# Two-block transformer kernel, one Trainium2 core: 36 of 44 up-projection pairs of the convolution feed-forward as seven half-size block products, with GpSimd making the weight sums, the gated product and its remainder

## The reference, cut to what matters

```python
def conv_ffn(h, w_up, conv_w, conv_b, w_down):
    u = h @ w_up                       # 512 x 1024 by 1024 x 5632
    u = lax.conv_general_dilated(u, conv_w[:, None, :], window_strides=(1,),
        padding=[(CONV_WIDTH - 1, 0)], feature_group_count=c, ...) + conv_b
    a, gate = jnp.split(u, 2, axis=-1)
    return (jax.nn.silu(gate) * a) @ w_down     # 512 x 2816 by 2816 x 1024
...
h = rms_norm_2(x, ffn_norm_g[layer])
x = x + conv_ffn(h, ffn_w_up[layer], ffn_conv_w[layer], ffn_conv_b[layer], ffn_w_down[layer])
```

## Time and profile before

| What | us |
|---|---|
| Time, median of 3 runs (lowest, highest) | 3203.16 (3202.86, 3203.87) |
| Span of the profiled execution, first to last instruction | 3201.8 |
| PE busy | 3186.1 |
| DVE busy | 1969.6 |
| ACT busy | 1271.3 |
| POOL busy | 404.6 |

### The profile page before, as it was taken

The page is one execution under the profiler, slowest core; times in us unless marked ns, Lnnn a source line. Parts: engine busy times, 40 slices in busy tenths (PEclk is TensorE's granted clock), DMA queues, the critical chain, the costliest instruction groups (busy, mean ns, idle before and its releaser), DMA issues.

```text
span 3201.8 us, 44978 instructions
## 1 busy us (share of the span) xinstructions
PE 3186.1 (100%) x16214; PEld 2672.4 (83%) x16214; DVE 1969.6 (62%) x2804; ACT 1271.3 (40%) x1734; POOL 404.6 (13%) x356
## 2 busy tenths in 40 slices
PE   9999999999999999999999999999999999999998
PEld 7788888889998788888889998768888888888887
DVE  8455567585557455557585555666665744585656
ACT  4433333334453433343334453254332523553423
POOL 2100000124221100000124221051000101320001
PEclk9999999999999999999999999999999999999999
DMA  7146324423323156324423322203222322122222
GB/s 267 67 167 206 126 94 167 140 92 106 106 99 106 55 169 208 121 98 166 142 87 106 106 99 83 86 21 112 99 99 93 105 99 92 47 85 100 92 99 79
DMA packets 100037, 359.24 MB, mean 112 GB/s; under 512 B 11056, under 2 KB 13360, under 8 KB 99760
## 3 DMA queue, kind: packets, MB, share of 16 engines
q1 hardware_dynamic: 98960, 354.08, 32.3%
q0 software_dynamic: 928, 3.17, 0.3%
HBM read 355.11 MB, written 2.10 MB: 112 GB/s over the span
## 4 chain that ended last, share of the span: by engine, by line
PE 94%; DVE 2%; POOLq 1%; issue 1%; ACT 1%; DVEq 1%; DMA 0%; ACTq 0%; SPq 0%; POOL 0%
PE pb L687 21%; PE pb L688 21%; PE pb L689 21%; PE pb L1002 6%; PE pb L719 2%; PE pb L720 2%; PE pb L723 2%; PE pb L759 2%; PE pb L757 2%; PE pb L758 2%; PE pb L1110 1%; PE pb L1485 1%; PE pb L1486 1%; PE pb L1487 1%; PE pb L978 1%
## 5 line engine op out<-in xcount | busy, mean ns | idle before, releaser
L1557 ACT ACTIVATE hi<-raw 128x1024 fp32r<-128x1024 f32 x500 | 524.8, 1056 | 850.0 <-PE pb L689 543.5
L2181 DVE TENSOR_TENSOR lo<-raw,hi 128x1024 fp32r<-128x1024 f32 (+1 forms) x500 | 617.6, 1241 | 330.1 <-ACT hi L1557 304.3
L687 PE MATMUL pb<-yH,hi 128*128 128x512 f32 (+1 forms) x1664 | 644.2, 387 | 0.0
L688 PE MATMUL pb<-yL,hi 128*128 128x512 f32 (+1 forms) x1664 | 644.0, 387 | 0.0
L689 PE MATMUL pb<-yH,lo 128*128 128x512 f32 (+1 forms) x1664 | 643.9, 387 | 0.0
L687 PE MATMUL pb<-hH,hi 128*128 128x512 f32 x1128 | 440.5, 391 | 0.0
L688 PE MATMUL pb<-hL,hi 128*128 128x512 f32 x1128 | 439.0, 389 | 0.0
L689 PE MATMUL pb<-hH,lo 128*128 128x512 f32 x1128 | 438.9, 389 | 0.0
L687 PEld LDWEIGHTS pb<-yH,hi 128*128 128x128 f32 x1664 | 312.5, 188 | 63.6
L689 PEld LDWEIGHTS pb<-yH,lo 128*128 128x128 f32 x1664 | 312.4, 188 | 63.5
L688 PEld LDWEIGHTS pb<-yL,hi 128*128 128x128 f32 x1664 | 312.5, 188 | 63.4
(11 more groups left out here) (486 smaller groups left out, 5237.5 us busy)
## 6 DMA issues: line engine op xcount, KB each, us to landing
raw<-stream SPq DMA_DIRECT2D x648, 512.0 KB, 3.3
yF<-first SPq DMA_DIRECT2D x8, 512.0 KB, 12.0
act<-first SPq DMA_DIRECT2D x8, 512.0 KB, 16.5
x<-xT SPq DMA_DIRECT2D x4, 512.0 KB, 7.6
outT<-act SPq DMA_DIRECT2D x7, 256.0 KB, 2.2
act<-crow POOLq DMA_DIRECT2D x2, 512.0 KB, 5.6
tab<-decay SPq DMA_DIRECT2D x1, 1024.0 KB, 7.8
scr<-ws POOLq DMA_DIRECT2D x2, 256.0 KB, 3.1
```

The lines of the kernel that those rows point to most:

```text
L687: pe.matmul(out, whi, ahi, start=first, stop=False)
L688: pe.matmul(out, whi, alo, start=False, stop=False)
L1557: act.activation(hi[:, s], raw[:, s], ACT.Copy).then_inc(hi_ready, 1)
L2181: dve.tensor_tensor(lo[:, s, 0:width], raw[:, s, 0:width], hi[:, s, 0:width].bitcast(F32), ALU.subtract).then_inc(lo_ready, 1)
```

## The change

`CONV_FAST = (4, 8, 6)` pairs at the end of the three slabs go through `conv_group` in place of two plain tiles: 18 pairs a layer, 36 in the kernel. The first 4 pairs of the first slab of a layer stay plain. In detail:

- **PE** runs `seven_products`, the routine of the first block's groups made general. It waits for `lo_ready` of the two tiles, for `e_lo` (the rest of the weight sums) and for `p_kept` (copies out of PSUM by ACT).
- **GpSimd** first makes the token sums (`conv_tokens`: 8 `tensor_scalar` of 512 columns and 16 `tensor_tensor` of 256). Then, for each fast pair, it makes four weight sums (`four_sums`, one of them in place in `raw`), and the product `a` by `gate` and the rest `midL` of the pair two back in its list, which were DVE's.
- **ACT** gets four copies of 256 columns out of PSUM for each fast pair and a rounding of 128x1536 sums, beside what it had.
- **DVE** gets the rest of the sums (128x1536), and two instructions for every plain one on PSUM: an addition that reads PSUM and then a multiplication by `rows`, SBUF by SBUF. It no longer makes the product nor `midL`, but for the last pair of a slab.
- The three `hi` and `lo` that a slab's down tiles start with are made at three places inside the last fast pair (`tick(1)`, `tick(2)`, `tick(3)`).

Buffers `ext` and `extR` are new (6 x 512 floats a partition), and the kernel asks for a `dynamic_dma_scratch_size` of 4096. The core of the diff, without the removed lines of the old `fast_group`:

```diff
+CONV_FAST = (4, 8, 6)
+FAST_1 = 2 * len(FAST_SLABS) * FAST_GROUPS
...
+        c_sum = lambda q: act3[:, 4:7] if q else ext[:, 0:3]
+        c_sumL = lambda q: halved[:, 4:7] if q else extR[:, 0:3]
+        c_sumH = lambda q: tabR[:, 1:4] if q else extR[:, 3:6]
+        c_kept = lambda q, i: scr[:, q * S + i * 256:q * S + (i + 1) * 256]
+        c_at = lambda layer, j, m: FAST_1 + layer * sum(CONV_FAST) + sum(CONV_FAST[:j]) + m - (SLABS[j] - CONV_FAST[j])
+        c_kept_at = lambda at: 3 * FAST_1 + 4 * (at - FAST_1)
...
+            def four_sums(at, n, sums):
+                if at >= 2:
+                    pool.wait_ge(p_full, 5 * (at - 1))
                 pool.tensor_tensor(e3, a11, a21, ALU.subtract)
                 pool.drain()
                 pool.tensor_tensor(a21, a21, a22, ALU.add)
...
+            def conv_pairs(layer):
+                conv_tokens(layer)
+                for j, n in enumerate(SLABS):
+                    first = n - CONV_FAST[j]
+                    def sums_of(m):
+                        e = c_sum(m % 2)
+                        four_sums(c_at(layer, j, m), c_tile(layer, j, m), [e[:, i] for i in range(3)])
+                    def product_of(m):
+                        pool.wait_ge(gated, layer * sum(SLABS) + sum(SLABS[:j]) + m + 1)
+                        p = A[:, 2 * m % RING]
+                        pool.tensor_tensor(p, p, A[:, 2 * m % RING + 1], ALU.mult)
+                        pool.drain().then_inc(product, 1)
+                        pool.wait_ge(product_hi, layer * (sum(SLABS) - 3) + sum(SLABS[:j]) - j + m + 1)
+                        pool.tensor_tensor(midL[:, m], p, midH[:, m].bitcast(F32), ALU.subtract)
+                        pool.drain().then_inc(y_ready, 1)
+                    sums_of(first)
+                    for m in range(first, n):
+                        if m + 1 < n:
+                            sums_of(m + 1)
+                        if m:
+                            product_of(m - 1)
...
+            def seven_products(at, q, banks_of, own, token, extra, kept_at, before_token=None, before_upper=None):
+                s0, s1 = 2 * q, 2 * q + 1
+                one_sum, other_sum, upper, lower_sum = (pb[:, b, 0:256] for b in banks_of)
                 pe.wait_ge(lo_ready, tiles.next())
                 pe.wait_ge(bank_free, banks.next(2))
+                product_of(one_sum, ring_part(s0, 0), own(0, 0)).then_inc(p_full, 1)
                 pe.wait_ge(lo_ready, tiles.next())
+                if before_token is not None:
+                    pe.wait_ge(t_lo, before_token)
+                product_of(other_sum, ring_part(s1, 0), token(1)).then_inc(p_full, 1)
+                if before_upper is not None:
+                    pe.wait_ge(y_ready, before_upper)
+                product_of(upper, ring_part(s0, 1), own(1, 0)).then_inc(tile_done, 1)
+                product_of(lower_sum, ring_part(s1, 1), token(4)).then_inc(tile_done, 1)
                 pe.wait_ge(e_lo, at + 1)
+                pe.wait_ge(p_kept, kept_at[0])
+                product_of(one_sum, extra(2), token(2), False).then_inc(p_full, 1)
+                pe.wait_ge(p_kept, kept_at[1])
+                product_of(other_sum, extra(4), own(1, 1), False).then_inc(p_full, 1)
+                pe.wait_ge(p_kept, kept_at[2])
+                product_of(one_sum, extra(3), token(3), False).then_inc(p_full, 1)
...
+            def conv_group(layer, j, m):
+                at, q = c_at(layer, j, m), m % 2
+                done_before = c_kept_at(at)
+                seven_products(at, q, (4 + 2 * q, 2 * q + 1, 2 * q, 5 + 2 * q),
+                               lambda k, t: (yH[:, KH[k], TH[t]], yL[:, KH[k], TH[t]]),
+                               lambda i: (c_tokH(i), c_tokL(i)),
+                               lambda i: (c_sumH(q)[:, i - 2], c_sumL(q)[:, i - 2]),
+                               (done_before + 1, done_before + 2, done_before + 4),
+                               LAYERS + layer + 1 if j == 0 else None)
...
+                    for m in range(plain, n):
+                        q = m % 2
+                        s0, s1 = 2 * q, 2 * q + 1
+                        keep(m, 0, c_kept(q, 0), 4 + 2 * q)
+                        if m + 1 < n:
+                            conv_hi(layer, j, m + 1, 0)
+                        else:
+                            tick(1)
+                        keep(m, 1, st[:, s1, TH[1]], s1)
+                        if m + 1 < n:
+                            conv_hi(layer, j, m + 1, 1)
+                        else:
+                            tick(2)
+                        if m:
+                            gate(m - 1)
+                        act.wait_ge(tile_done, done.next(2))
+                        act.activation(st[:, s1, TH[0]], pb[:, 5 + 2 * q, TH[0]], ACT.Copy).then_inc(p_kept, 1)
+                        keep(m, 2, c_kept(q, 1), 4 + 2 * q)
+                        if m + 1 < n:
+                            conv_hi(layer, j, m + 1, 2)
+                        else:
+                            tick(3)
+                        if m:
+                            product_rounded(m - 1)
+                        if m >= 2:
+                            act.wait_ge(y_ready, c_mid(layer, j, m - 1))
+                        step(m, 0)
+                        step(m, 1)
...
+                    for m in range(plain, n):
+                        at, q = c_at(layer, j, m), m % 2
+                        s0, s1 = 2 * q, 2 * q + 1
+                        if m + 1 < n:
+                            conv_lo(layer, j, m + 1)
+                        else:
+                            tick(1)
+                            tick(2)
+                        dve.wait_ge(p_kept, c_kept_at(at) + 4)
+                        dve.wait_ge(tile_done, done.next(2))
+                        dve.wait_ge(p_full, 5 * at + 4)
+                        u = st[:, s0]
+                        dve.tensor_tensor(u.rearrange("p (t s) -> p t s", t=2), pb[:, s0:s1 + 1, 0:256],
+                                          scr[:, q * S:(q + 1) * S].rearrange("p (t s) -> p t s", t=2), ALU.add)
+                        dve.drain()
+                        dve.tensor_tensor(u, u, rows, ALU.mult)
+                        dve.drain().then_inc(u_ready, 1)
+                        if m + 1 < n:
+                            conv_sum_lo(layer, j, m + 1)
+                        else:
+                            tick(3)
+                        dve.wait_ge(p_full, 5 * at + 5)
+                        xs, u = pb[:, 4 + 2 * q, 0:256], st[:, s1]
+                        xx = bass.AP(xs.tensor, xs.offset, [xs.ap[0], (0, 2), (1, 256)])
+                        both = u.rearrange("p (t s) -> p t s", t=2)
+                        dve.tensor_tensor(both, xx, both, ALU.add).then_inc(bank_free, 2)
+                        dve.drain()
+                        dve.tensor_tensor(u, u, rows, ALU.mult)
+                        dve.drain().then_inc(u_ready, 1)
+                        drained.next(2)
+                        taps(m, 0)
+                        taps(m, 1)
```

More of the change, by code:

```diff
@@ L985, in first_tiles_halved, with product_of @@
                 tile_T(3, hH, hL)
+            ring_part = lambda s, k: [w[:, s, k * S:(k + 1) * S] for w in (hi, lo)]
+            def product_of(out, weights, tokens, first=True):
+                (wH, wL), (aH, aL) = weights, tokens
+                for k in range(4):
+                    w = slice(k * P, (k + 1) * P)
+                    for n, (wP, aP) in enumerate(((wH, aH), (wH, aL), (wL, aH))):
+                        ins = pe.matmul(out, wP[:, w], aP[:, k], start=first and k == n == 0, stop=k == 3 and n == 2,
+                                        skip_group_check=not first)
+                return ins
@@ new lines, in keep @@
+                    def keep(m, i, to, bank):
+                        act.wait_ge(p_full, 5 * c_at(layer, j, m) + i + 1)
+                        act.activation(to, pb[:, bank, 0:256], ACT.Copy).then_inc(p_kept, 1)
+                    for i in range(2 * plain):
+                        m = i // 2
+                        done.next()
+                        if i + RING < 2 * plain:
+                            tick((i + 1) % RING)
+                        elif i == RING:
+                            act.wait_ge(t_sums, LAYERS + layer + 1)
+                            for t in (1, 2, 3, 4):
+                                act.activation(c_tokH(t), c_raw_token(t), ACT.Copy)
+                            act.drain().then_inc(t_hi, 1)
+                        elif i == RING + 1:
+                            conv_hi(layer, j, plain, 0)
+                            conv_hi(layer, j, plain, 1)
+                        elif i == RING + 2:
+                            conv_hi(layer, j, plain, 2)
+                        if i % 2 == 0 and m:
+                            gate(m - 1)
+                        step(m, i % 2)
+                        if i % 2 == 0 and m:
```

(10 more changed lines are left out.)

209 lines of the change are left out of this document (127 added, 82 removed).

## The result

The changed kernel takes 3358.74 us (median of 4 runs, 3356.98 to 3360.65) against 3203.26 us (3202.86 to 3203.87) for the kernel before, measured beside it: ratio 1.0485, 95% interval 1.0471 to 1.0500. It is 155 us slower; the forecast was 113 us slower (its sum gave 113.8), with a range of 3280 to 3385. The profiled span is 3358.5 us.

A forecast was written before the change was run, and what follows sets the result against it. PE bounds the kernel before; in fast pairs DVE and POOL taking turns would. Per layer 18 x 14.63 - 2 x 5.3 = 252.7 us replaces 195.8; both layers add 113.8, rounded to 113, giving 3316 us, range 3280 to 3385.

The forecast's parts named there:

- What bounds a fast pair: Convolution fast pairs: DVE and POOL taking turns on SBUF set the pair's time, and PE waits some 4.5 us a pair.
- DVE alone, 10.47 us: DVE's instructions for one fast pair, with nothing waited for, sum to 10.47 us, against PE's 10.07.
- A turn of POOL, 1.05 us: Fast pairs: each of POOL's six instructions holds the shared SBUF side for 1.05 us, whole instructions in turn with DVE's.
- the pair, 14.63 us: A fast pair: DVE 7.85, POOL 6.30 and drains 0.48 together take 14.63 us, against 10.88 before.
- Ends of the slabs: Starts and ends of slabs 2 and 3, where all pairs are fast: each slab costs 14.63 n less 5.3 us.
- -5.3: Slabs 2 and 3: correction per slab, -4.8 us plus another 0.5 off because PE begins with its banks free.
- Slab 1, taken as 0 beyond its 4 x 3.75: Slab 1 of each layer: preparing work of 46 us against 43.5 us of plain pairs, taken as 0; slab forecast +15.0 us.
- First rival, no hindrance: Fast pairs: DVE and POOL hardly hinder each other; PE gains 29 us, slab-end waits cost 18; net -8, 3195 us; chance 0.10.
- Second rival, the clock: Fast pairs: PE's idle time drops its clock to 1.2 GHz; about 3366 us, up to 3475; chance 0.12.
- Signs named beforehand: Trace after: groups every 14.6 us, DVE's taps and `lo` about 1 us longer beside POOL, PE idle before fifth and seventh products.

The follow-up runs named there:

- e_tap_less: The changed kernel with the last of the four DVE convolution taps left out of each fast pair: 3324.46 us.
- e_pe_less: The changed kernel with the third matmul of each group of three left out of the fast pairs' seven products (28 of 84 matmuls a pair): 3348.66 us.
- e_small_pool: The changed kernel with the six POOL instructions of a fast pair on 32 of 512 columns: 3231.79 us.
- e_two_set: The changed kernel with two more POOL memsets of 512 columns ahead of the first weight sum of each fast pair: 3363.8 us.
- e_no_pool: The changed kernel with token sums left out and the fast pairs' six POOL instructions on 32 of 512 columns: 3213.88 us.

## Why the prediction was right, and where it was off

**What bounds a fast pair.** Right. DVE is the path through the fast pairs (e_tap_less against e_pe_less), and what makes it so is POOL (e_small_pool: 127 of 155 us; memsets in e_two_set, which take POOL's time but no turn, leave the period).

**DVE alone, 10.47 us.** Right: 10.58 measured once POOL is out of the way.

**A turn of POOL, 1.05 us, and the pair, 14.63 us.** Right in sum: 14.85. The order of the turns that I wrote out was not the one that came, and the parts differ: six turns cost DVE 4.33 us more length, two of them being mostly under the additions from PSUM, and one costs 0.82 to 1.10 where it does fall on DVE. The forecast of a pair is 0.22 us too low.

**Ends of the slabs.** Here two errors work against each other, which is luck: without that the miss would be larger. The formula gives the fast pairs 14.63 us each less the -5.3; with the short last intervals PE is through them in 483.9 us over the six slabs and not 505.5, 21.6 less. Against it the first three down tiles of the six slabs take 32.6 us more than before, for which the sum had no term, though its own first rival priced the wait there at 18 us. About 22 of the 32.6 are waits (3.5 to 3.9 us a slab, most of it for a bank freed by L3072), the other 0.2 to 2.7 a slab are matmuls at the lower clock. With the 32.5 us by which the first waits exceed the usual spacing of matmuls, -21.6 + 32.6 + 32.5 is the missing 43.

**Slab 1, taken as 0 beyond its 4 x 3.75.** This is the step that failed, by 34 of the 43 us; the first waits are 33 us. Three things in it, in the order of their size. The token sums: I counted 16 half-size instructions at half a turn, 8.4 us, and left out the eight multiplications by the gain ahead of them, 1.55 us each even where DVE is idle, and treated POOL's work as turns only. It is 31 us of POOL in a row, and POOL's own length was on the path; it cost 6.9 and 10.7 us. The weight sums of the first two fast pairs, which POOL makes right behind: 3.8 us a layer; I had counted their turns against a slab with 43.5 us of room, but they come when that room is over. What stays without POOL: 3.5 us a layer. The sum's 46 us over 43.5, rounded down to 0, does not explain it: without the token sums' 8.4 and the weight sums' 4.2 it holds 33.4, and in e_no_pool DVE is busy for 28 of the slab's first 44 us. The amount would have fitted; what counts is its place in DVE's list: the rests stand behind the sixth of the eight plain tiles, the `lo` behind the seventh. In the trace all this shows as one wait on PE, and ACT and DVE stood in it too.

**First rival, no hindrance.** Out as to the cause. Yet its estimate of what is left without POOL, -8 us, is tested too: e_no_pool has +10.8. Over the six slabs the fast pairs gain 12 us on the plain ones and not 29, since DVE bounds them at 10.6 to 10.7 us (the rival took off 3 for that); the first three down tiles cost 15.8, near its 18; and the first waits, which it did not have, are 7.1.

**Second rival, the clock.** The lower level did come, in short stretches (a granted clock of 0.92 in the steady window), and it cost nothing there, as the rival says for up to half a pair. It costs where PE is not held up by DVE, which the rival did not look at. These are the matmuls 0.43 us apart in the first down tiles: some 10.5 us over the six slabs, the clock's part of the 155. At slab 1's start it slows the first product, 2.7 us in place of 1.44 in both layers.

**Signs named beforehand.** Groups of matmuls every 14.6 us: 14.85. `lo` and taps about 1 us longer: `lo` and two of the four taps. POOL's sums at 1.8 to 2.8 us: one at 2.62, the others at 1.43 to 1.79. PSUM additions at 0.69: 0.68. PE idle ahead of the fifth and seventh product: yes, 0.3 to 2.4 us and 0.2 to 1.9 in slab 2, though it was always an ACT copy (`p_kept`) that came last, also where I had named `e_lo`. PE's spacing of 0.12: not behind these waits, where it is 0.21 in some products.

## What to carry to other kernels

Where VectorE and GpSimd work side by side, count GpSimd's instructions that read SBUF and price each at VectorE's cost of a turn (0.86 us here for 512 fp32 columns), whatever share of the time GpSimd is busy; then look for VectorE instructions with an input in PSUM that they can lie under, for these are free. Price the steady pair and the preparation ahead of it apart: the preparation is a chain through all engines, and there the length of each engine's own work counts, not only what it takes from a neighbour. Fewer matmuls pay only when the engine that feeds them has the time: here 0.81 us a pair on TensorE was bought with DVE work that left 0.3 us of room even without GpSimd.

## What the runs showed of the hardware

- A turn belongs to a whole instruction: 32 columns on POOL took 1.62 us against a DVE instruction of 1.76 us and 0.25 us without one.
- POOL memsets take no turn from DVE (1.76 us beside two of them). A one-input copy costs about half of what a two-input sum does (0.48 against 0.86 us of the period), and is about half as long (0.61 against 1.29 us).
- DVE's additions and multiplications with one input in PSUM, of 512 columns, run at 0.68 to 0.70 us in these pairs whatever POOL does.
- On POOL a multiplication of 512 fp32 columns by a scalar from memory takes 1.55 us, longer than a two-input sum of the same size, 1.29.
- TensorE at the lower clock cost nothing inside the pairs (granted clock 0.76 in e_pe_less, 10 us faster) and some 10.5 us in the first down tiles of the six slabs (matmuls 0.43 us apart in place of 0.23), where the rows show no wait.
